# Fp32 decoder trunk on one core: the last chunk of each block of x turned by VectorE and carried through DRAM

## The reference

```python
for i in range(2):
    g = norm_gains[i]
    h = rmsnorm(x, g[0])
    y = swa_sink_attention(h, ...) if i == 0 else forgetting_attention(h, ...)
    x = x + rmsnorm(y, g[1])
    h = rmsnorm(x, g[2])
    y = swiglu_ffn(h, ffn_w_gate_up[i], ffn_w_down[i])
    x = x + rmsnorm(y, g[3])
```

## Time and profile before

| | |
|---|---|
| median of 3 runs | 2127.19 us (2126.78 to 2127.22) |
| the profiled execution, its own time | 2127.44 us |
| its span, first to last instruction | 2125.5 us |
| mean granted TensorE clock | 0.999 of full speed |
| TensorE, VectorE, ScalarE, GpSimd busy | 2115.1, 1587.3, 1180.5, 121.0 us |
| DMA | 399.85 MB, mean 188 GB/s |

### The profile page before, as it was taken

One profiled execution on the slowest core, in us unless ns is written; L12 is line 12 of the kernel. 1 busy time (PEld: TensorE's weight loads), 2 busy tenths in 40 slices (PEclk: granted clock), 3 DMA queues, 4 the chain that ended last, 5 costly groups with the idle time before them and its releaser, 6 DMA issues.

```text
span 2125.5 us, 32513 instructions
## 1 busy us (share of the span) xinstructions
PE 2115.1 (100%) x9795; PEld 1735.5 (82%) x9795; DVE 1587.3 (75%) x3257; ACT 1180.5 (56%) x2133; POOL 121.0 (6%) x231
## 2 busy tenths in 40 slices
PE   9999999999999999999999999999999999999998
PEld 7877888888888888888878877888888888888886
DVE  6777577877668876678787777577776778776786
ACT  7776565544555444555676566565454555445453
POOL 2111000000000000000231131000000000000000
PEclk9999999999999999999999999999999999999999
DMA  7544856555666655665665664666655665556652
GB/s 259 189 139 133 215 180 219 187 188 177 203 211 190 195 172 193 197 206 156 185 197 182 181 195 160 207 199 198 198 174 182 197 216 187 187 179 198 216 186 91
DMA packets 205692, 399.85 MB, mean 188 GB/s; under 512 B 13248, under 2 KB 13664, under 8 KB 205104
## 3 DMA queue, kind: packets, MB, share of 16 engines
q1 hardware_dynamic: 203008, 389.86, 58.6%
q0 software_dynamic: 2320, 8.72, 1.4%
q10 hardware_dynamic: 288, 0.33, 0.0%
HBM read 396.72 MB, written 2.13 MB: 188 GB/s over the span
## 4 chain that ended last, share of the span: by engine, by line
PE 98%; DVE 1%; issue 1%; DMA 0%; POOL 0%; ACT 0%; SPq 0%; POOLq 0%; DVEq 0%; ACTq 0%
PE bank L1233 31%; PE bank L1235 31%; PE bank L1234 31%; PE bank L1282 1%; PE bank L1309 1%; PE bank L1293 1%; PE bank L1246 1%; DMA x_sb<-x 0%; PE bank L1265 0%; DVE ring_lo L759 0%; DVE x_sb L802 0%; DVE y_sb L1027 0%; POOL post_r L1126 0%; DVE a_lo L766 0%; DVE y_sb L795 0%
## 5 line engine op out<-in xcount | busy, mean ns | idle before, releaser
L1233 PE MATMUL bank<-ring_hi,a_hi 128*128 128x512 f32 x2240 | 884.0, 395 | 0.6 <-DVE ring_lo L759 0.6
L1235 PE MATMUL bank<-ring_hi,a_lo 128*128 128x512 f32 x2240 | 873.2, 390 | 0.0
L1234 PE MATMUL bank<-ring_lo,a_hi 128*128 128x512 f32 x2240 | 872.1, 389 | 0.0
L557 ACT ACTIVATE ring_hi<-stage,g_t 128x512 fp32r<-128x512 f32 x992 | 663.2, 717 | 340.1 <-DMA stage<-ffn_w_gate_up 202.4
L759 DVE SCALAR_TENSOR_TENSOR ring_lo<-stage,g_t,ring_hi 128x512 fp32r<-128x512 f32 x992 | 708.8, 760 | 162.1 <-ACT ring_hi L557 160.1
L1235 PEld LDWEIGHTS bank<-ring_hi,a_lo 128*128 128x128 f32 x2240 | 420.4, 188 | 88.8
L1233 PEld LDWEIGHTS bank<-ring_hi,a_hi 128*128 128x128 f32 x2240 | 420.6, 188 | 88.2 <-issue 4.1
L1234 PEld LDWEIGHTS bank<-ring_lo,a_hi 128*128 128x128 f32 x2240 | 421.0, 188 | 83.4
L757 DVE TENSOR_TENSOR ring_lo<-stage,ring_hi 128x512 fp32r<-128x512 f32 x480 | 306.7, 690 | 131.5 <-ACT ring_hi L555 130.2
L555 ACT ACTIVATE ring_hi<-stage 128x512 fp32r<-128x512 f32 x480 | 277.3, 624 | 167.7 <-PE bank L1235 150.0
L1233 PE MATMUL bank<-ring_hi,h_hi 128*128 128x512 f32 x704 | 274.4, 390 | 0.0
(11 more groups left out here) (144 smaller groups left out, 855.8 us busy)
## 6 DMA issues: line engine op xcount, KB each, us to landing
stage<-ffn_w_gate_up SPq DMA_DIRECT2D x352, 512.0 KB, 4.6
stage<-ffn_w_down SPq DMA_DIRECT2D x176, 512.0 KB, 5.6
stage<-fox_w_in SPq DMA_DIRECT2D x96, 512.0 KB, 4.1
stage<-swa_w_in SPq DMA_DIRECT2D x48, 512.0 KB, 4.5
stage<-swa_w_out SPq DMA_DIRECT2D x64, 256.0 KB, 4.1
stage<-fox_w_out SPq DMA_DIRECT2D x32, 512.0 KB, 4.6
g_b<-norm_gains POOLq DMA_DIRECT2D x4, 1024.0 KB, 5.9
cum_b<-cum_scratch POOLq DMA_DIRECT2D x32, 128.0 KB, 3.4
```

The lines of the kernel that those rows point to most:

```text
L557: nc.scalar.activation(ring_hi[:, n % RING, :], src, ACT.Identity, scale=g_t[:, row * KT + j:row * KT + j + 1]).then_inc(hi_ready, 1)
L1233: nc.tensor.matmul(dst, hi_a, hi_w, start=start, stop=False)
L1234: nc.tensor.matmul(dst, hi_a, lo_w, start=False, stop=False)
L1235: return nc.tensor.matmul(dst, lo_a, hi_w, start=False, stop=stop)
```

## The change

For the last chunk (q = 3) of each block, at b = 1, 2 and 3, TensorE's four transposes are left out. In their place:

- `turn_x` on VectorE (step 21 of the last unit for block 0, step 5 of the next unit for block 1): one transpose instruction over 128x512 that turns each 32x32 block in its place, from `x_sb` into `x_blocks`. All six uses have the one buffer `x_blocks`, so from the second on it waits for the store before it.
- `carry_x` on GpSimd: a store of `x_blocks` to DRAM (256 KB), a wait for it to land, and four loads, each of which brings one group of 32 partitions of `x_f[t]` in runs of 512 bytes. `carry_x(b, 0)` stands between `post(b, 0)` (at b = 2: behind the load of `fg_raw`) and `post(b, 1)`; `carry_x(b, 1)` behind `post(b, 1)`, ahead of the two `rstd`.
- heads and rests of chunk 3 are made from `x_f[t]` in SBUF. Those of (0, 3) move from steps 28 and 30 of the last unit (b = 2: step 31 and step 0 of the next unit) to steps 9 and 10 of the next; those of (1, 3) from steps 18 and 20 (b = 2: 19) to 25 and 26.
- the order of the counting semaphores follows (`x_order`), and `x_squares` waits for the sums and not for the transposes.

```diff
-X0_STEPS = {1: (22, 24, 26, 28), 2: (25, 27, 29, 31), 3: (22, 24, 26, 28)}
-X0_REST_STEPS = {1: (24, 26, 28, 30), 2: (27, 29, 31, 32), 3: (24, 26, 28, 30)}
+X0_STEPS = {1: (22, 24, 26), 2: (25, 27, 29), 3: (22, 24, 26)}
+X0_REST_STEPS = {1: (24, 26, 28), 2: (27, 29, 31), 3: (24, 26, 28)}
+X_TURNED = (21, 5)
+LAST_HEADS = (41, 25)
+LAST_RESTS = (42, 26)
-X_STEPS = {1: (8, 11, 14, 18), 2: (9, 12, 14, 18), 3: (8, 11, 14, 18)}
-X_REST_STEPS = {1: (10, 13, 16, 20), 2: (10, 13, 15, 19), 3: (10, 13, 16, 20)}
+X_STEPS = {1: (8, 11, 14), 2: (9, 12, 14), 3: (8, 11, 14)}
+X_REST_STEPS = {1: (10, 13, 16), 2: (10, 13, 15), 3: (10, 13, 16)}
...
+            def turn_x(b, t):
+                dve.wait_ge(x_new, 8 * (b - 1) + 4 * t + NC_D)
+                if (b, t) != (1, 0):
+                    dve.wait_ge(x_stored, 16 * (2 * (b - 1) + t))
+                nc.vector.transpose(x_blocks[:, :, :].rearrange("p b (k i) -> p k b i", i=Q),
+                                    x_sb[:, t, col(NC_D - 1)].rearrange("p (k b j) -> p k b j", b=P // Q, j=Q)).then_inc(x_turned, 1)
...
                         if s in X_REST_STEPS[b]:
                             x_rests(b, 1, X_REST_STEPS[b].index(s))
+                        if s == LAST_RESTS[0] - STEPS:
+                            x_rests(b, 0, NC_D - 1)
+                        if s == LAST_RESTS[1]:
+                            x_rests(b, 1, NC_D - 1)
...
+            def carry_x(b, t):
+                n = 2 * (b - 1) + t + 1
+                pool.wait_ge(x_turned, n)
+                pool.dma_start(x_dram[t], x_blocks[:, :, :].rearrange("p b r -> p (b r)")).then_inc(x_stored, 16)
+                pool.wait_ge(x_stored, 16 * n)
+                blocks = x_dram[t].rearrange("(a j) (b r) -> b j a r", a=P // Q, b=P // Q)
+                for b in range(P // Q):
+                    pool.dma_start(x_f[t][Q * b:Q * (b + 1), :, :, :].rearrange("p a k i -> p a (k i)"), blocks[b]).then_inc(xf_loaded[t], 16)
...
                         pool.dma_start(fg_raw[:, :, :], ...).then_inc(fg_loaded, 16)
+                    if b < 4:
+                        carry_x(b, 0)
                     post(b, 1)
                     if b < 4:
+                        carry_x(b, 1)
                         for t in range(NT):
                             rstd(pre_ms, pre_r, t, pre_mean, 2 * b + t + 1, pre_rstd)
```

More of the change, by code:

```diff
@@ L198, in build @@
         cum_b = at("cum_b", 44 * KB + 256, [P, 4, SEQ])
+        x_blocks = at("x_blocks", 12 * KB, [P, P // Q, 4 * Q])
+        x_f = [at(f"x_f{t}", (40 + 2 * t) * KB, [P, P // Q, 4, Q]) for t in range(NT)]
         y_sb = at("y_sb", 16 * KB, [P, NT, D])
@@ L254, in build @@
         biased, stored = sem("biased"), sem("stored")
+        x_turned, x_stored = sem("x_turned"), sem("x_stored")
+        xf_loaded = [sem(f"xf_loaded{t}") for t in range(NT)]
         diag_made, pe_summed, pe_read, pe_stored = sem("diag_made"), sem("pe_summed"), sem("pe_read"), sem("pe_stored")
+        x_dram = [nc.dram_tensor(f"x_scratch{t}", (P, CH), F32, kind="Internal").ap() for t in range(NT)]
         cum_dram = nc.dram_tensor("cum_scratch", (NH, SEQ), F32, kind="Internal").ap()
@@ L322, in wait_stg_turned @@
                 eng.wait_ge(qk_turned, 2 * c + (0 if part == 0 else 1) + 2 * i)
+        X_SECOND = {b: [c for _, c in sorted([(s, (1, q)) for q, s in enumerate(X_STEPS[b])] + [(LAST_HEADS[0] - STEPS, (0, 3)), (LAST_HEADS[1], (1, 3))],
+                                               key=lambda step: step[0])]
+                    for b in (1, 2, 3)}
         def tok(t):
@@ L478, in x_part, with turned_by_dma, x_transposed, x_order @@
             return NT * NC_D * b + k, x_ps[k % NC_D]
+        def turned_by_dma(b, q):
+            return b > 0 and q == NC_D - 1
+        def x_transposed(b, t, q):
+            if turned_by_dma(b, q):
+                return x_f[t][:, :, :, :].rearrange("p a k i -> p k a i")
+            return x_part(b, t, q)[1][:, :].rearrange("p (k a i) -> p k a i", k=4, i=Q)
+        def x_order(b, t, q):
+            if b == 0:
+                return x_part(0, t, q)[0]
+            first = [(0, 0), (0, 1), (0, 2)] + X_SECOND[b]
+            return 8 * b + first.index((t, q))
+        def wait_x_transposed(eng, b, t, q):
+            if turned_by_dma(b, q):
+                eng.wait_ge(xf_loaded[t], 64 * b)
+            else:
+                eng.wait_ge(xt_done, (8 + 6 * (b - 1) + 3 * t + q if b else x_part(0, t, q)[0]) + 1)
         def y_gain_count(b, t, q):
@@ L560, in x_heads @@
             def x_heads(b, t, q):
[L562 to L565, removed]
+                wait_x_transposed(act, b, t, q)
+                nc.scalar.activation(a_hi[:, 4 * q:4 * q + 4, tok(t)].rearrange("p k (a i) -> p k a i", i=Q),
+                                     x_transposed(b, t, q), ACT.Identity).then_inc(xt_hi, 1)
             def x_squares(b, t):
-                act.wait_ge(xt_done, x_part(b, t, NC_D - 1)[0] + 1)
+                act.wait_ge(x_new, 8 * (b - 1) + 4 * t + NC_D)
                 nc.scalar.activation(y_sb[:, t, :], x_sb[:, t, :], ACT.Square, accum_out=xsq[:, t:t + 1]).then_inc(x_squared, 1)
@@ L709, in unit @@
                             x_heads(b, 1, X_STEPS[b].index(s))
+                        if s == LAST_HEADS[0] - STEPS:
+                            x_heads(b, 0, NC_D - 1)
+                        if s == LAST_HEADS[1]:
+                            x_heads(b, 1, NC_D - 1)
                         if s in (14, 25):
@@ L762, in x_rests @@
             def x_rests(b, t, q):
[L763 to L766, removed]
+                dve.wait_ge(xt_hi, x_order(b, t, q) + 1)
+                hi = a_hi[:, 4 * q:4 * q + 4, tok(t)].bitcast(F32).rearrange("p k (a i) -> p k a i", i=Q)
+                nc.vector.tensor_tensor(a_lo[:, 4 * q:4 * q + 4, tok(t)].rearrange("p k (a i) -> p k a i", i=Q), x_transposed(b, t, q),
                                         hi, ALU.subtract).then_inc(xt_lo, 1)
+            def turn_x(b, t):
[4 more added lines that the diff above has]
+                                    x_sb[:, t, col(NC_D - 1)].rearrange("p (k b j) -> p k b j", b=P // Q, j=Q)).then_inc(x_turned, 1)
             def x_mean(b, t):
@@ L933, in unit @@
                             residual_sum(b, 0, s - 17)
+                        if b < 4 and s == X_TURNED[0]:
+                            turn_x(b, 0)
                         if b % 2 == 0 and s in Y_GAIN_STEPS[b]:
@@ L946, in unit @@
                             residual_sum(b, 1, s - 1)
+                        if s == X_TURNED[1]:
+                            turn_x(b, 1)
                         if s in X_REST_STEPS[b]:
                             x_rests(b, 1, X_REST_STEPS[b].index(s))
+                        if s == LAST_RESTS[0] - STEPS:
+                            x_rests(b, 0, NC_D - 1)
+                        if s == LAST_RESTS[1]:
+                            x_rests(b, 1, NC_D - 1)
                         if s in (18, 27):
@@ L1240, in transpose_x @@
                     pe.wait_ge(x_loaded[n], 16)
+                    if n >= 4:
+                        pe.wait_ge(xt_lo, n - 3)
                 else:
                     pe.wait_ge(x_new, 8 * (b - 1) + 4 * t + q + 1)
-                if n >= 4:
-                    pe.wait_ge(xt_lo, n - 3)
+                    pe.wait_ge(xt_lo, x_order(b, 0, q) + 1 if t else 8 * b)
                 for k in range(4):
@@ L1352, in input_block @@
                 if b is not None and j % 4 == 0:
-                    pe.wait_ge(xt_lo, x_part(b, t, j // 4)[0] + 1)
+                    pe.wait_ge(xt_lo, x_order(b, t, j // 4) + 1)
                 if out_chunk(u) in (0, 1) and j % 2 == 0:
```

## The result

The changed kernel takes 2138.63 us (median of 5 runs, 2136.83 to 2140.01) against 2127.22 (5 runs, 2126.78 to 2127.84): ratio 1.0052, 95% interval 1.0041 to 1.0063. That is 11.4 us slower. 2137.2 was forecast, with a range of 2132.2 to 2141.3.

What follows compares the result with a forecast made beforehand. TensorE was taken to bound the kernel, busy 2115.1 of 2125.5 us. Passages 1 and 3 at 0.9 each, passage 2 at 6.2 and the clock at 2.0 sum to +10.0, giving 2137.2 us, range 2132.2 to 2141.3.

Steps and rivals of the forecast that it cites:

- What leaves TensorE: Transposes of six chunks left out on TensorE at passages 1 to 3: 0.44 us each, 2.65 us gained in all.
- The turning: VectorE's transpose of 128x512: 0.70 us, or 0.61 with overlap, if 128 partitions cost what 32 do.
- VectorE's order: Passages 1 to 3: rests of (0, 3) queue late on VectorE, so step 12 starts 7.27 us after the first sum.
- GpSimd, mis-sized: Passages 1 and 3: store and wait take 4.9 us, GpSimd is 0.7 late, each passage costs +0.9 us.
- GpSimd at passage 2: Carrying queues behind the load of fg_raw: post(2, 1) starts at 1005.42, where it was 1003.33; first sum at 1006.4.
- The clock: Passage 2: TensorE's idle times bring the clock to 1.2 GHz, costing +2.0 us, bounds 0 and 2.8.
- The sum of passage 2: Step 12 starts 6.66 us later, less 0.44 for (1, 3), giving +6.2; the clock adds +2.0.
- A: Rival at passage 2: the sum holds but the clock stays up, +8.0 us, 2135.2; chance 0.24.
- B: Rival: GpSimd isn't late, VectorE's order alone costs +5.3 us; 2132.5 to 2134.5 with part of the clock; chance 0.1.
- C: Rival: carrying is much slower, heads of (0, 3) late, (1, 3) misses step 28; +4 to +8 more, 2141 to 2145; chance 0.08.
- D: Rival: VectorE reaches rests of (0, 3) ahead of TensorE's step 12; -2.65 to -3.4 us, 2123.8 to 2124.5; chance 0.03.
- E: Rival: VectorE's turning takes 2.8 us, adding 8.8 us over passages 1 to 3; 2146; chance 0.05.

Runs made afterwards that it cites:

- The kernel of the last experiment: Changed kernel with passage 2 back on TensorE and rests of (0, 3) at step 7 at passages 1 and 3: 2125.46 us, ratio 0.9991.
- the fillings: Changed kernel with extra matmuls of unused result in the two waits of passage 2: 2139.41 us; with fewer of them, 2134.84 us.
- the fitted filling: Changed kernel with unused matmuls cut to what passage 2's two waits hold, 10 and 17 calls: 2134.84 us, ratio 1.0038.
- the carrying-first kernel: Changed kernel with block 0's carrying right behind post(b, 0), at passage 2 ahead of the load of fg_raw: 2135.49 us, ratio 1.0038.
- the early orders: Carrying-first kernel with heads and rests of chunk 3 at earlier steps: 2136.52 us; the same with passage 2 on TensorE: 2132.08 us.
- the kernel with the late rests: Kernel before the change with only the rests of (0, 3) moved to step 10 of the next unit: 2131.73 us, ratio 1.0021.
- the kernel with the early order: Carrying-first kernel with chunk 3's heads and rests at earlier steps, all six chunks carried: 2136.52 us, ratio 1.0043.

## Why the prediction was right, and where its terms were off

- **What leaves TensorE**: 24 matmuls fewer, at 0.44 us a chunk. The kernel of the last experiment gains 1.2 by the spans and 1.8 by the medians for four chunks (1.76) less a wait of 0.46. Right.
- **The turning**: 0.705 us for 128x512, 0.70 forecast from two sizes on 32 partitions. So 128 partitions cost what 32 do.
- **VectorE's order**: from the first sum to step 12 it takes 277.06 to 284.39 and 1006.02 to 1013.35, 7.33 both times; 7.27 forecast. Shown as the cause by the kernel before with one subtraction moved, and by the kernel that doesn't carry.
- **GpSimd, mis-sized**: a store and its wait took 4.10 us at passage 1 and 4.20 at passage 3, not 4.9. `post(1, 1)` started 0.24 us behind the start of the mean's last instruction (275.83 to 276.07), just as in the earlier trace rows of before, so it wasn't late at all; at passage 3 it was 0.13 late. Forecast was 0.7. So these passages cost 0.20 and 0.29, not 0.9 each; that is the lower bound that was given (0.3). The two forecast waits of 1.8 at step 12 are listed with 0.96 and 0.97 (1.2 at passage 1 by the starts, as the forecast reckons).
- **GpSimd at passage 2**: `post` started at 1005.42, to the hundredth as forecast, and that is luck. The forecast moved the load of `fg_raw` 0.44 earlier for the transposes of (0, 3) that are gone, but these stand behind step 31, and the load waits for the matmuls of step 31 only: the store was issued at 998.45 and not at 998.15. Store, wait and loads then took 6.95 us in place of 7.22. And from `post` to the first sum it was 0.60 us and not 0.98, so the sum came at 1006.02 where 1006.4 was forecast.
- **Step 0 at passage 2, no term of the sum**: `turn_x(2, 0)` stands ahead of the rests of (0, 0) in VectorE's queue. They ended at 997.27, TensorE started step 0 at 997.37 and had waited 0.42 for them; a second turning made that 1.01. It cost nothing in the total, since TensorE waited for the sums nine steps later anyway, but together with the earlier sum it made that wait shorter: 2.4 us where 3.4 was forecast.
- **The clock**: it fell, as forecast. From step 12 to the first matmul behind the transposes of (1, 2) TensorE took 1018.65 - 1013.35 = 5.30 us where it took 2.86 before, +2.44; 2.0 forecast. The forecast took the low level's price from the start of the span by the spacing of the matmuls (0.24 us each; the same ones took 0.115 in the fillings), while the profile lists a granted clock of 1.00 for that stretch, so there the spacing and the listed clock disagree. The Trainium skill, page "TensorE: Matmul & The Clock Gate", Part 1, has low activity halve the clock; the trace agrees, with 0.52 and 0.50 granted.
- **Step 28 at passage 2, no term of the sum**: the prediction found under 1 us to spare, without showing how, and had no term for it; TensorE stood 1.05 us longer than between neighbours (1027.39 to 1028.67, less 0.23). The heads of (1, 3) stand behind the reading of the first projection on ScalarE, and that waits for a chain: squares of x, VectorE's weight tile of step 16, the mean, GpSimd's `rstd`. This is read from the trace; no run moved these heads alone. That it is neither the clock nor the data is shown by the runs with the clock up and without the carrying, which wait 0.90 and 0.88. The rows (ScalarE, VectorE, VectorE, GpSimd, ScalarE, ScalarE):

```profile
1019.43 1.91 ACT L606 ACTIVATE y_sb<-x_sb 128x2048 f32<-128x2048 f32 x1
...
1022.07 0.75 DVE L799 SCALAR_TENSOR_TENSOR ring_lo<-stage,g_t,ring_hi 128x512 fp32r<-128x512 f32 x1 [1.81 <-ACT ring_hi L594]
1022.73 0.15 DVE L823 TENSOR_SCALAR pre_ms<-xsq 128x1 f32<-128x1 f32 x1
...
1022.97 0.57 POOL L1181 TENSOR_TENSOR pre_r<-pre_ms,half_pow 128x1 f32<-128x1 f32 x1 [5.37 <-DVE pre_ms L823]
...
1023.62 0.69 ACT L636 ACTIVATE stg<-bank,pre_r 128x512 f32<-128x512 f32 x1 [1.59 <-issue]
1024.21 3.17 ACT L594 ACTIVATE ring_hi<-stage,g_t 128x512 fp32r<-128x512 f32 x5
1027.27 0.62 ACT L600 ACTIVATE a_hi<-x_f 128x512 fp32r<-128x512 f32 x1
```

- **The sum of passage 2**: step 12 is 1013.35 - 1007.01 = 6.34 later than in the earlier trace rows, and 6.46 with the 0.12 that the kernel was ahead; + 2.44 (clock) + 1.05 (step 28) - 0.44 (transposes of (1, 3)) = 9.51 of the 9.63 measured. Forecast were 6.66 + 2.0 - 0.44 = 8.2.
- **The whole**: +10.0 forecast, +9.8 in the profiled execution. The terms that were too high (1.3 at passages 1 and 3) and too low (1.4 at passage 2) cancel; that the total is better than its parts is luck. The median is 11.4 over that of before, and the changed kernel scatters over 3.2 us where the other scatters over 1.1. Its two longest runs (2139.52, 2140.01) list a mean granted clock of 0.996, the other three 0.997, and the version with its clock held up scatters over 1.5; that suggests the clock, but this wasn't separated.
- **The rivals**: A (clock up) and B (GpSimd in time) are what the fitted filling and the carrying-first kernel are, and both still lose about 8; neither cause alone carries the loss. C (late loads) was not at work here but is real, as the early orders show, and it was near: at passage 1 the last load, issued at 275.5, landed after 6.2 us at 281.7 and not at 279.9, and ScalarE read it at 282.08. D (not slower) fell with the waits: the rests of (0, 3) ended at 284.25 and 1013.2. E fell with 0.705 us.

Not tried: the carrying by another engine's queue, the in-between place (step 7) at passage 2, and at passage 2 block 0 alone.

## What to carry to other kernels

When TensorE is the bound, a piece of work taken off it comes back if a step that feeds it is put at the end of another engine's queue: add up what stands ahead of that step in the queue, from the event that releases the queue, and compare with the start of its reader; the new operation's own length (0.7 us here) is the small part. A wait of 3.3 to 4.5 us on TensorE, as these runs had it, also costs part of what follows it, through the clock. And a step moved forward again must not pass the landing of its data, or an in-order engine carries the DMA's latency on to everything behind it: the good place (step 7) lay between one that loses (step 4) and one that gains nothing (step 10).

## What the runs showed of the hardware

- A load of 64 KB by GpSimd landed after 3.6 us in the median and 6.2 at most (24 loads). The slowest two groups of four were those of block 0 at passages 1 and 3 (4.1 to 6.2), in flight with the DMA engines 90% and 85% busy (273.8 to 277.8, 1405 to 1409). But four loads at passage 2 landed after 3.4 to 3.8 with 85% (1015.4 to 1018.4), so this share alone doesn't tell.
- A store of 256 KB to DRAM by GpSimd took 3.8 to 4.5 us to land. By the fit in the Trainium skill, page "DMA: Bandwidth & Descriptors", section "Anatomy of one DMA — SWDGE (gpsimd) path", an estimate is 2.6 us; the measurement decides. Neither size nor the writing alone makes the difference: SyncE's stores of 256 KB at the end of the span landed after 2.4.
- Behind a wait of 3.3 us at step 12, in the kernel with the late rests, the granted clock was 0.78 over 1011 to 1018 us, with TensorE busy all the time. In the kernel with the early order it stayed at 1.00 behind waits of 2.3, 2.8 and 2.2 us.
